# Gates of three mixers turned by VectorE in 32x32 blocks instead of by TensorE, and the banks of the output projections exchanged

## The reference, cut to what matters

```python
proj = jnp.einsum('bsd,dc->bsc', h, w_in[layer])
...
gate = proj[..., 3 * MIX_WIDTH:4 * MIX_WIDTH]
...
y = jnp.stack([o_a, o_b, o_c, o_d], axis=1)
y = y.transpose(0, 3, 1, 2, 4).reshape(bsz, seq, MIX_WIDTH)
y = y * jax.nn.silu(gate)
x = x + jnp.einsum('bsc,cd->bsd', y, w_out[layer])
```

## Time and profile before

| | us |
|---|---|
| median of 3 runs | 2974.82 (2974.67 to 2977.38) |
| the profiled execution | 2974.32 |
| its span, first to last instruction | 2972.5 |
| PE busy | 2961.2 |
| DVE busy | 1946.3 |
| ACT busy | 1466.9 |
| POOL busy | 287.1 |

### The profile page before, as it was taken

How to read it: one execution, slowest core, us unless ns; L and a number is a source line. 1 busy time by engine, 2 the same in 40 slices (tenths; PEclk the granted TensorE clock), 3 DMA queues, 4 the chain that set the end, 5 groups by cost and what they waited for, 6 DMA issues and landing times.

```text
span 2972.5 us, 37941 instructions
## 1 busy us (share of the span) xinstructions
PE 2961.2 (100%) x13766; PEld 2428.7 (82%) x13766; DVE 1946.3 (65%) x2360; ACT 1466.9 (49%) x1832; POOL 287.1 (10%) x265
## 2 busy tenths in 40 slices
PE   9999999999999999999999999999999999999999
PEld 7888888888888778888888888888777888877787
DVE  6666766766557868657666756667556587755654
ACT  6654444444445555544444444455555545555553
POOL 0110000000005421100000000004300000510000
PEclk9999999999999999999999999999999999999999
DMA  7766666666666446666666666666555556655555
GB/s 258 237 185 194 192 191 195 193 190 196 193 193 198 144 135 208 190 192 194 188 197 194 192 193 191 197 193 193 161 153 153 159 187 184 185 156 149 159 160 171
DMA packets 281231, 549.42 MB, mean 185 GB/s; under 512 B 16928, under 2 KB 19760, under 8 KB 280720
## 3 DMA queue, kind: packets, MB, share of 16 engines
q1 hardware_dynamic: 276928, 531.45, 59.0%
q0 software_dynamic: 4176, 16.26, 1.5%
HBM read 540.82 MB, written 6.82 MB: 184 GB/s over the span
## 4 chain that ended last, share of the span: by engine, by line
PE 97%; ACT 1%; DVE 1%; DMA 1%; issue 0%; POOL 0%; SPq 0%; ACTq 0%; DVEq 0%; POOLq 0%
PE ps L494 24%; PE ps L1013 21%; PE ps L550 15%; PE ps L502 12%; PE ps L1020 11%; PE ps L521 7%; PE ps L1166 1%; PE ps L1233 1%; PE ps L1141 1%; PE ps L1266 1%; PE ps L827 0%; ACT w_hi L403 0%; PE ps L768 0%; PE ps L1294 0%; DMA w_raw<-xattn_w_kv 0%
## 5 line engine op out<-in xcount | busy, mean ns | idle before, releaser
L410 DVE TENSOR_TENSOR w_lo<-w_raw,w_hi 128x1024 fp32r<-128x1024 f32 x1008 | 1254.6, 1248 | 952.5 <-ACT w_hi L403 943.1
L403 ACT ACTIVATE w_hi<-w_raw 128x1024 fp32r<-128x1024 f32 x1008 | 1066.5, 1059 | 1370.9 <-PE ps L502 546.7
L1013 PE MATMUL ps<-w_hi,actT_hi 128*128 128x512 f32 x1408 | 548.1, 389 | 0.0
L1013 PE MATMUL ps<-w_hi,actT_lo 128*128 128x512 f32 x1408 | 547.8, 389 | 0.0
L550 PE MATMUL ps<-w_hi,actT_hi 128*128 128x512 f32 x960 | 389.9, 406 | 1.4 <-ACT pall L574 1.4
L1020 PE MATMUL ps<-w_lo,actT_hi 128*128 128x512 f32 x1408 | 376.3, 389 | 0.0
L550 PE MATMUL ps<-w_hi,actT_lo 128*128 128x512 f32 x960 | 375.3, 391 | 0.0
L494 PE MATMUL ps<-w_hi,hidT_hi 128*128 128x512 f32 x864 | 318.7, 390 | 0.8 <-DVE hidT_hi L1322 0.8
L1013 PEld LDWEIGHTS ps<-w_hi,actT_hi 128*128 128x128 f32 x1408 | 264.4, 188 | 54.8
L1020 PEld LDWEIGHTS ps<-w_lo,actT_hi 128*128 128x128 f32 x1408 | 264.3, 188 | 54.9
L1013 PEld LDWEIGHTS ps<-w_hi,actT_lo 128*128 128x128 f32 x1408 | 264.2, 188 | 54.8
(11 more groups left out here) (310 smaller groups left out, 3115.3 us busy)
## 6 DMA issues: line engine op xcount, KB each, us to landing
w_raw<-ffn_w_in SPq DMA_DIRECT2D x352, 512.0 KB, 4.2
w_raw<-w_in SPq DMA_DIRECT2D x256, 512.0 KB, 3.6
w_raw<-ffn_w_out SPq DMA_DIRECT2D x176, 512.0 KB, 4.7
w_raw<-w_out SPq DMA_DIRECT2D x64, 512.0 KB, 4.2
w_raw<-attn_w_in SPq DMA_DIRECT2D x48, 512.0 KB, 3.9
w_raw<-xattn_w_kv SPq DMA_DIRECT2D x32, 512.0 KB, 6.5
w_raw<-attn_w_out SPq DMA_DIRECT2D x32, 512.0 KB, 4.0
w_raw<-xattn_w_q SPq DMA_DIRECT2D x16, 512.0 KB, 4.0
```

What stands on the lines that cost most here:

```text
L403: nc.scalar.activation(w_hi[:, v % NS], w_raw[:, v % NS], ACT.Copy).then_inc(w_hi_done, 1)
L410: nc.vector.tensor_tensor(w_lo[:, v % NS], w_raw[:, v % NS], w_hi[:, v % NS].bitcast(F32), ALU.subtract).then_inc(w_lo_done, 1)
L1013: nc.tensor.matmul(ps[:, 2 * b + tb], lhs[:, k, tb * P:(tb + 1) * P], w_hi[:, s, kk * CB:(kk + 1) * CB], start=(k == 0 and part == 0), sto ...
```

## The change

The turns of gates 0, 1 and 2 leave PE. DVE transposes each gate in four quarters of four instructions (32 partitions by 256 elements), from the projection's home to `yT_raw`, that is from SBUF to SBUF. The quarters of the gates stand in positions 74, 75, 77, 78; 82, 83, 85, 86; and 89, 91, 92, 93. The waits that PE had for the gates are now DVE's. The products with the mixers' outputs read `yT_raw` and write it in place, now in positions 88, 90 and 94; the rounding and the low parts follow one position later, as before. The gate of mixer 3 is still turned by PE.

`out0` and `out1` use the halves 1, 0, 1, 0. The wait for the last rows of `rest` moves from the first to the second block of `out`. The semaphores in `dve_last` and in SP's stores of the result follow.

```diff
         def half_of(name, b):
-            return (b + (name == "aout")) % 2
+            return (b + (name in ("aout", "out0", "out1"))) % 2
...
                 dve.wait_ge(w_used, used)
-                nc.vector.tensor_tensor(xb, xb, acc(b % 2), ALU.add).then_inc(acc_free[b % 2], 1)
+                half = half_of(name, b)
+                nc.vector.tensor_tensor(xb, xb, acc(half), ALU.add).then_inc(acc_free[half], 1)
...
-            if pos_ in Y_TURNS:
-                t = Y_TURNS.index(pos_)
+        def dve_gate_quarter(dve, l, t, a):
+            if a == 0:
                 if t == 1:
-                    pe.wait_ge(row_free[1], in_rest(l, 13))
+                    dve.wait_ge(row_free[1], in_rest(l, 13))
                 else:
-                    pe.wait_ge(y_gated, 2 * l + t // 2 + 1)
-                pe_turn(pe, f"y{l}", pall, o_done, units[-1]["group"] + 1, part=(2 * t, 2 * t + 2))
+                    dve.wait_ge(y_gated, 2 * l + t // 2 + 1)
+            for f in range(4):
+                ins = nc.vector.transpose(
+                    yT_raw[32 * f:32 * f + 32, 4 * t:4 * t + 4].rearrange("p k (h t) -> p h k t", h=TB)
+                    [:, :, :, 32 * a:32 * a + 32],
+                    proj(3, t)[32 * a:32 * a + 32].rearrange("p h (k n) -> p h k n", k=4)[:, :, :, 32 * f:32 * f + 32])
+            if a == 3:
+                ins.then_inc(t_done, 2)
...
-            nc.vector.tensor_tensor(yT_raw[:, 4 * t:4 * t + 4], ps[:, b:b + 2].rearrange("p b (k t) -> p (b k) t", k=2),
-                                    out_home(t), ALU.mult).then_inc(y_made, 1)
+            gate = ps[:, b:b + 2].rearrange("p b (k t) -> p (b k) t", k=2) if t == 3 else yT_raw[:, 4 * t:4 * t + 4]
+            nc.vector.tensor_tensor(yT_raw[:, 4 * t:4 * t + 4], gate, out_home(t), ALU.mult).then_inc(y_made, 1)
...
-        Y_TURNS = (90, 92, 94)
+        GATE_QUARTERS = ((74, 75, 77, 78), (82, 83, 85, 86), (89, 91, 92, 93))
+        Y_TURNS = (88, 90, 94)
...
                 dve_out(dve, units[SCORED.index(pos_ - 4)])
+            for t in range(3):
+                if pos_ in GATE_QUARTERS[t]:
+                    dve_gate_quarter(dve, l, t, GATE_QUARTERS[t].index(pos_))
...
                 pe_linear(pe, f"out{l}", tiles(yT_hi), tiles(yT_lo), t_lo_done, ready_of(f"y{l}"), rows=ROWS[f"rest{l}"] + NREST,
-                          turned="in1" if l == 0 else None)
+                          rows_at=1, turned="in1" if l == 0 else None)
```

More of the change, by code:

```diff
@@ L968, in evac @@
                         dve.wait_ge(done, n)
-                        nc.vector.tensor_tensor(xb[:, tb], xb[:, tb], acc(b % 2)[:, tb], ALU.add).then_inc(last_in[tb], 1)
+                        nc.vector.tensor_tensor(xb[:, tb], xb[:, tb], acc(half_of(name, b))[:, tb], ALU.add).then_inc(last_in[tb], 1)
                     return
                 dve.wait_ge(w_used, used)
-                nc.vector.tensor_tensor(xb, xb, acc(b % 2), ALU.add).then_inc(acc_free[b % 2], 1)
+                half = half_of(name, b)
+                nc.vector.tensor_tensor(xb, xb, acc(half), ALU.add).then_inc(acc_free[half], 1)
             split_turns(dve, dve_split, name, evac)
@@ L2135, in _ @@
             for b in range(3):
-                sp.wait_ge(acc_free[b % 2], h_[b % 2] + b // 2 + 1)
+                half = half_of("out1", b % 2)
+                sp.wait_ge(acc_free[half], h_[half] + b // 2 + 1)
                 sp.dma_start(out_rows[:, :, b * CB:(b + 1) * CB], x[:, :, b * CB:(b + 1) * CB]).then_inc(x_out, 16)
```

## The result

| | before | after |
|---|---|---|
| median of 20 runs each, us | 2974.74 | 2980.79 |
| the profiled execution, us | 2974.32 | 2981.23 |
| its span, us | 2972.5 | 2979.4 |

The ratio of the runs is 1.0019, with a 95% interval of 1.0013 to 1.0025: the changed kernel is 6.05 us slower by the medians (0.20%), where 4.4 were forecast. One of its 20 runs took 3270.88 us at a clock of 0.851; it is not in the ratio, and without it the median is 2980.70 and the difference 5.96 us.

A forecast was written before the change was run, and what follows sets the result against it. PE was taken as the bound, busy all but 11 us of the span. Per layer 2.1 - 0.72 = 1.4 us slower, 2.8 in both, plus 1.6 at `qk1`: 4.4 slower, 2979.2 us; range 2969.5 to 2984.0, the forecast's own 2977 to 2981.5.

The forecast's parts named there:

- The turns and the seam: On PE: six turns removed at 0.89 us each, and 0.62 us of wait removed at each start of `out`.
- The price of a transpose: On DVE, SBUF to SBUF: one 32x256 transpose taken as 456 ns, bounds 295 and 500.
- rival A: DVE's transposes within SBUF run at the faster rate: 4.8 us faster, 2970.0; chance 14%.
- The scores: Positions 76 and 84: quarters ahead delay the score 1.54 us; 1.05 us reach PE each, 2.1 us per layer.
- about 1.3 us: Sign to look for: PE waiting this long for L574's copy at the ends of rows 79 and 87.
- Rival C: At the scores, ACT finds time to give back, so the lag misses PE: 0.2 us slower, 2975.0; chance 12%.
- The rule on held instructions: DVE's quarters: each costs the longer time, 1.87 us, not 1.76; shorter first quarters would make the sum 0.6 us less.
- The wait for gate 3: Two units into `out`: PE waits some 2.5 us for DVE's scaling; DVE's work from the split of 89 sums to 22.96.
- `qk1`: Start of `qk1`: PE starts about 1.6 us later, once, as DVE is still adding out its banks; bounds 1.4 and 1.8.
- Rival D: The seam of `out0` costs nothing because another wait there is relieved: 2977.6; chance 3%.
- of 3.3 us only 0.72 is kept: Two units into `out`, per layer: PE comes 3.3 us sooner but waits for DVE's scaling, keeping 0.72 us.
- rival B: Transposes are dearer: loss passes 0.2% (5.95 us) at 480 ns, 2982.0 at 500 ns; same two waits; chance 21%.

The follow-up runs named there:

- the spread quarters: Changed kernel with quarters of gates 0 and 1 at positions 74, 77, 78, 79 and 82, 85, 86, 87: 2975.09 us, ratio 1.000; traced again, 2973.34 us.
- the later turn: Changed kernel with PE's turn of gate 3 behind unit 2 of `out` instead of unit 1, its product and low part one position later: 2972.62 us, ratio 0.9994.
- the banks as before: Changed kernel with the exchange of banks undone, `out0` and `out1` using halves 0, 1, 0, 1 again: 2976.84 us, ratio 1.0006.
- the first batch: Runs of four variants of the changed kernel (wait filled, turn later, banks undone, quarters spread) sharing runs of the kernel before, whose median was 2974.68 us.

## Why the prediction was right, step by step

The sign, the places and the mechanism held: 2979.2 us with +4.4 against 2980.79 with +6.05, within the forecast's own range of 2977 to 2981.5. The near hit is in part two misses of opposite sign: about 1.4 us too much in the steps that were forecast, above all the waits, and 3.3 us left out for the clock. That the sum came out near is in part luck: whether the clock falls differs from run to run, and without any fall the steps add up to +2.96 us, some 2977.7, which would have been inside that range too. The one run of the changed kernel with a clock of 1.000 took 2977.98 us.

*The turns and the seam: right.* -0.90 per turn against 0.89, -0.62 per seam against 0.62.

*The price of a transpose: mis-sized.* I took 456 ns, the row with a PSUM target. From SBUF to SBUF they take (shortest, median, longest, in the view of the tile):

```profile
L1710 DVE STREAM_TRANSPOSE yT_raw<-pall x96: 425/436/444, 2312.4 to 2885.0; 32x256 f32<-32x256 f32 x96
```

436 ns is near the row I took, and far from 295: rival A fell. The single rate of the Trainium skill's "Vector Engine (DVE) Microarchitecture Reference", section 3.8, agrees with this; the double rate that "VectorE: DVE Perf Modes" gives copies does not reach the transpose.

*The scores: right in mechanism, 0.2 us too dear each.* DVE at positions 74 to 76 and ACT behind it, to be held against the earlier trace rows:

```profile
2311.26 1.23 DVE L410 TENSOR_TENSOR w_lo<-w_raw,w_hi 128x1024 fp32r<-128x1024 f32 x1 [2.69 <-ACT w_hi L403]
2312.40 1.78 DVE L1710 STREAM_TRANSPOSE yT_raw<-pall 32x256 f32<-32x256 f32 x4
2314.19 1.23 DVE L410 TENSOR_TENSOR w_lo<-w_raw,w_hi 128x1024 fp32r<-128x1024 f32 x1
2315.45 1.78 DVE L1710 STREAM_TRANSPOSE yT_raw<-pall 32x256 f32<-32x256 f32 x4
2317.24 1.23 DVE L410 TENSOR_TENSOR w_lo<-w_raw,w_hi 128x1024 fp32r<-128x1024 f32 x1
2318.39 1.22 DVE L1181 SCALAR_TENSOR_TENSOR S<-ps,causal 128x1024 f32<-128x1024 f32 x1
...
2320.89 0.51 ACT L1211 ACTIVATE S<-S,nmx 128x256 f32<-128x256 f32 x1 [0.68 <-DVE nmx L1184]
...
2327.07 0.47 PE L550 MATMUL ps<-w_hi,actT_hi 128*128 128x512 f32 x1 [0.80 <-ACT pall L574]
```

From the split of 74 to the score it is 7.13 us: the working had 7.40, the kernel before 5.86. Two quarters at 1.79 instead of 1.87 and a first split of 1.14 instead of 1.26 are the 0.27. The score is 1.27 us late instead of 1.54, less ACT's 0.5 of slack is 0.8, and PE has 0.82. (The working's 1.05 is itself a little high: 2320.47 less 2319.45 is 1.02. And its sign of "about 1.3 us" of waiting at these places came out as 0.80.) Rival C said that ACT gives it back; it gave nothing.

*The rule on held instructions: the trace agrees.* A split takes 1.23 us; the quarter of strip 0 starts 1.14 behind it (2311.26 to 2312.40), beside its end, that of strip 1 after 1.26 (2314.19 to 2315.45), behind it. And what follows a quarter never starts before its end (1.79 after 1.78), while with a target in PSUM it could. That is what the Trainium skill, "VectorE: DVE Perf Modes", "Two Vector instructions with no wait between them", says of start quadrants that differ. My working charged the hold to every first split too.

*The wait for gate 3: right, 0.25 us too long.* DVE runs with hardly a gap from the split of 89 at 2363.91 to the end of the scaling at 2385.34 + 1.22 = 2386.56: 22.65 us where the working had 22.96. Four quarters at 1.89 instead of 1.99 with their splits are 0.4 less; the last low part, behind ACT, takes 0.1 of that back. PE goes on 0.10 us later. Of 3.3 us it kept 0.99, not 0.72.

*`qk1`: right.* 1.70 against 1.6, of which 1.37 us is idleness; the rest is overlap with the matmul ahead that is lost, and 0.17 us within the unit behind. Rival D, that another wait there would be relieved, fell.

*The step that failed* is in the same point: "of 3.3 us only 0.72 is kept". It counted the wait as time that was free anyway, and priced the unit behind it at 2.72 us, as every other. It took 4.4. That the loss reached rival B's size (6 us) is not due to dearer transposes, which were cheaper (436 ns); 3.3 us of it are the granted clock.

## What to carry to other kernels

When work is taken off the bounding engine ahead of a fixed wait for another engine, reckon when the other engine is done first: the freed time goes into that wait, and here it came back with a surcharge for the clock. Before moving work to an engine with average room, look for the positions at which others read its results: 3.2 us of waits vanished by moving six of a layer's twelve quarters by one or two positions. A trade of a wait at one seam for a wait at the next is to be made only at those seams that have nothing waiting next (here one of two).

## What the runs showed of the hardware

TensorE's granted clock fell from 1.00 to about 0.5 (the 1.2 GHz level) around the idle time of 2.2 us ahead of the turn of gate 3, amid work that otherwise never stops: the matmuls behind it started 0.42 instead of 0.227 us apart for about 3.4 us, at a cost of 1.57 to 1.68 us. It fell behind 7 of 10 such idle times, behind both of 4.9 us (at least 6.7 us at the low level, 2.8 us of cost), and behind none of 1.6 us (two, one kernel) or of 1.4 us (at `qk1`, in the ten traces with that wait).

The same traces hold idle times of this length at two other places. In the kernel with the spread quarters PE stands idle for 2.26 us at 1197 us, in the kernel with the later turn for 2.58 us at the start of the kernel, where it waits for a load; the clock fell behind neither. Each timeline row is followed by the window behind it:

```profile
1199.25 1.99 PE L1167 MATMUL ps<-qkT 128*128 128x256 f32 x8 [2.26 <-ACT qkT L1151]
1200.00:1203.00 3.00, 3.00 (x15) 2.52 (x14) 2.53 (x3) 1.66 (x2) 0.00 (x0) 1.00 0.72 248
...
8.94 0.66 PE L768 MATMUL ps<-ident,mem_s 128*128 128x128 f32 x4 [2.58 <-DMA mem_s<-mem]
9.00:12.40 3.40, 3.40 (x18) 2.83 (x19) 2.98 (x4) 2.05 (x4) 0.00 (x0) 1.00 1.06 399
```

At the start there are eight idle times of 2.05 to 2.58 us, one in each of eight traces, and the clock fell behind five of them. The start is not quite the same case, since PE is not steadily busy ahead of that wait. The one of 2.30 us, with the banks as before:

```profile
9.20 1.10 PE L768 MATMUL ps<-ident,mem_s 128*128 128x128 f32 x4 [2.30 <-DMA mem_s<-mem]
9.00:12.70 3.70, 3.50 (x11) 2.92 (x12) 2.59 (x4) 2.33 (x4) 0.00 (x0) 0.54 1.04 396
```

With these, it fell behind 12 of 19 idle times of 2.05 to 2.58 us, and not behind the longest. Part of the scatter of all these kernels is this: in the first batch seven of the 31 runs of the kernel before show 0.999 (2975.64 to 2978.01 us), the others 1.000 (2973.49 to 2976.29 us).

The Trainium skill, "TensorE: Matmul & The Clock Gate", Part 1, names the two levels, and says that the ramp at a kernel's start differs from run to run of the same kernel. The levels and the difference from run to run can be seen here in mid-run as well. The length of the idle time alone does not decide whether some 2.2 us of it is too much; what does, no run here shows.
